# First two weight tiles of four projections take each normalised chunk together

## What is computed

```
def swiglu(x, w13, w2):
    gate, up = jnp.split(x @ w13, 2, axis=-1)
    return (jax.nn.silu(gate) * up) @ w2
...
x = layer_norm(DEEPNORM_ALPHA * x + (1.0 + g_m) * y, ln_mix_g[i], ln_mix_b[i])
u = x * (1.0 + sc_f) + sh_f
y = swiglu(u, ffn_w13[j], ffn_w2[j])
...
x = x + mod_l[5] * swiglu_2(modulate(rms_norm(x, norm2_w[i]), mod_l[3], mod_l[4]), ffn_w1[i], ffn_w3[i], ffn_w2[i])
```

## Time and profile before

| | |
|---|---|
| three executions | 2711.41, 2708.13, 2701.3 us |
| profiled execution, span (the page gives no other time for it) | 2713.5 us |
| PE busy | 2625.8 us, 97% |
| POOL, DVE, ACT busy | 910.4, 909.8, 404.2 us |
| mean granted PE clock | 0.989 |

### The profile page before, as it was taken

The page is one execution under the profiler, slowest core; times in us unless marked ns, Lnnn a source line. Parts: engine busy times, 40 slices in busy tenths (PEclk is TensorE's granted clock), DMA queues, the critical chain, the costliest instruction groups (busy, mean ns, idle before and its releaser), DMA issues.

```text
span 2713.5 us, 47220 instructions
## 1 busy us (share of the span) xinstructions
PE 2625.8 (97%) x20645; PEld 1863.1 (69%) x20645; DVE 909.8 (34%) x1647; ACT 404.2 (15%) x839; POOL 910.4 (34%) x715
## 2 busy tenths in 40 slices
PE   8999999989999999999999999999999999999998
PEld 6767799956644444334445446488888778998998
DVE  4746422384300011100013583222221136522651
ACT  0132010120311000100002344100000121221000
POOL 2662168584000000000000350145555331612886
PEclk9999999999999999999999999999999999999999
DMA  9978545478499999999997210323222243122552
GB/s 299 320 250 287 135 162 164 149 264 280 156 376 407 407 381 385 391 399 406 385 384 249 79 38 16 124 78 93 80 83 86 89 129 109 58 67 93 171 163 87
DMA packets 318303, 561.88 MB, mean 207 GB/s; under 512 B 45544, under 2 KB 181520, under 8 KB 317968
## 3 DMA queue, kind: packets, MB, share of 16 engines
q1 hardware_dynamic: 299280, 554.57, 57.4%
q10 hardware_dynamic: 18816, 4.27, 0.8%
HBM read 557.75 MB, written 1.05 MB: 206 GB/s over the span
## 4 chain that ended last, share of the span: by engine, by line
PE 50%; issue 36%; POOLq 4%; POOL 4%; DVE 2%; DVEq 1%; ACT 1%; DMA 1%; SPq 0%; ACTq 0%
PE psum L1937 10%; PE psum L2166 5%; PE psum L1974 5%; PE psum L2020 4%; PE psum L1021 3%; PE psum L1406 3%; PE psum L2194 2%; PE psum L1359 2%; PE psum L2040 2%; PE psum L1753 2%; POOLq L3767 2%; PE psum L1419 1%; PE psum L2067 1%; PE psum L1244 1%; PE psum L1062 1%
## 5 line engine op out<-in xcount | busy, mean ns | idle before, releaser
L1614 PE MATMUL psum<-ring,xe 128*32 128x512 f32 (+1 forms) x4608 | 458.0, 557 | 2.0 <-issue 1.4
L1614 PEld LDWEIGHTS psum<-ring,xe 128*32 128x32 f32 x4608 | 156.4, 110 | 291.1 <-issue 255.4
L3906 POOL TENSOR_TENSOR ckv<-ckv,nstat 128x512 f32<-128x512 f32 x2 | 2.5, 1265 | 889.9 <-DVE nstat L3413 889.9
L3304 DVE TENSOR_TENSOR act_in<-act_in,psum 128x256 f32<-128x256 f32 (+1 forms) x72 | 28.7, 399 | 629.5 <-ACT act_in L2474 629.5
L1636 PE MATMUL psum<-ring,zs 128*32 128x256 f32 x4224 | 232.3, 379 | 0.2 <-DMA ring<-in_moe_w 0.2
L1636 PEld LDWEIGHTS psum<-ring,zs 128*32 128x32 f32 x4224 | 141.7, 110 | 92.7 <-issue 5.5
L3919 POOL TENSOR_TENSOR w_sums<-ring 128x512 f32<-128x512 f32 (+1 forms) x34 | 42.4, 1247 | 298.1 <-DVE ctxT L3470 124.1
L2474 ACT ACTIVATE act_in<-psum 128x256 f32<-128x256 f32 (+1 forms) x72 | 26.4, 367 | 567.9 <-PE psum L1614 567.9
L1753 PE MATMUL psum<-a,ring 128*128 128x512 f32 x224 | 97.5, 594 | 2.0 <-ACT a L2523 1.3
L3413 DVE RECIPROCAL nstat<-nstat 128x512 f32<-128x512 f32 x23 | 75.8, 3328 | 43.0 <-ACT nstat L2235 43.0
L1937 PE MATMUL psum<-a,w_sums 128*128 128x256 f32 x352 | 83.2, 379 | 2.0 <-ACT a L2523 2.0
(11 more groups left out here) (612 smaller groups left out, 4892.6 us busy)
## 6 DMA issues: line engine op xcount, KB each, us to landing
ring<-in_moe_w SPq DMA_DIRECT2D x216, 1024.0 KB, 11.2
ring<-in_ffn_w SPq DMA_DIRECT2D x97, 1024.0 KB, 5.2
ring<-in_ada_w SPq DMA_DIRECT2D x96, 1024.0 KB, 8.4
ring<-in_moe_w SPq DMA_DIRECT2D x64, 768.0 KB, 6.6
ring<-in_hg_w_in SPq DMA_DIRECT2D x20, 1024.0 KB, 5.1
ring<-in_mlstm_w_in SPq DMA_DIRECT2D x16, 1024.0 KB, 9.2
ring<-in_mlstm_w_out SPq DMA_DIRECT2D x8, 1024.0 KB, 7.7
ring<-in_s_w_glu SPq DMA_DIRECT2D x8, 1024.0 KB, 11.7
```

What stands on the lines that cost most here:

```text
L1614: last = pe.matmul(psum[rows, r, 0:2 * nb * 32].rearrange("p (u b f) -> p u b f", u=2, b=nb), xe[:, k, at:at + 32], tile[:, :, :, rows], s ...
```

## The change

The first two weight tiles of the four projections are interleaved: PE waits for a chunk and multiplies it with tile 0 and tile 1 before it waits for the next. In `ffn0` all of tiles 0 and 1 is done so. In `ffn2` and `hg` products 1, 2 and 3 of both tiles are, and in `ffn3` products 1 and 2; the remaining products of tile 0 follow, then those of tile 1. The spare products between chunks are gone. Tile 1 of `ffn3` writes to other banks. On ACT the SiLU of tile 0 of `ffn0` now stands ahead of the S5 exponentials, and on DVE the product of gate and up ahead of the S5 parameters.

```diff
         def gate_up_side3(n):
-            return 2 * ((n + 1 - (job_of["rms3"] + 2) % NB // 2) % 2)
+            return NB if n == 1 else 2 * ((n + 1 - (job_of["rms3"] + 2) % NB // 2) % 2)
...
-                for n in range(2):
-                    mm_pair(ffn_tile(n), ffn_job(n), lambda k: act_in[:, k],
-                            before=None if n else lambda k: pe.wait_ge(S("ffn0_in_ready"), k + 1))
+                def first_tiles():
+                    for n in range(2):
+                        wait_tile(pe, ffn_tile(n))
+                        wait_free(pe, ffn_job(n))
+                    for k in range(DC):
+                        pe.wait_ge(S("ffn0_in_ready"), k + 1)
+                        for n in range(2):
+                            for b in range(2):
+                                at = k * 2 * P + b * P
+                                last = pe.matmul(bank(ffn_job(n))[:, b * T:(b + 1) * T], ring[:, ffn_tile(n) % RING, at:at + P],
+                                                 act_in[:, k], start=k == 0 and b == 0, stop=k == DC - 1, skip_group_check=True)
+                                if b == 0 and k == n * (DC - 1):
+                                    last.then_inc(tile_begun, 1)
+                            if k == DC - 1:
+                                full(last, ffn_job(n))
...
+                def first_two():
+                    for n in range(2):
+                        wait_tile(pe, t0 + n)
+                    for m in (1, 2, 3):
+                        if m == 3:
+                            pe.wait_ge(S("w_sums_ready"), INPUT_TILES - PLAIN_TILES + FF_SEVENS + 2)
+                            pe.wait_ge(S("a2_ctx_ready"), 16)
+                        for k in range(4):
+                            if m != 3:
+                                pe.wait_ge(S("a2_lat_ready"), 8 + (0 if m == 1 else 4) + k + 1)
+                            for n in range(2):
+                                last = product(n, m, k)
...
+                    for n in range(2):
+                        for m in (5, 6, 7, 4):
+                            if n == 0:
+                                pe.wait_ge(S("x_sums_ready"), 4 + 4 + {5: 1, 6: 2, 7: 3, 4: 4}[m])
+                            elif m == 6:
+                                pe.wait_ge(S("gap_mods_out"), 2)
+                            for k in range(4):
+                                last = product(n, m, k)
...
-                            if n == 0 and (m, k) in ((1, 2), (2, 0)):
-                                spare_products(product_bank(1, 1)[:, 0:P], 3 if m == 1 else 7)
...
-                s5_exponentials()
                 wait_full(act, ffn_job(0))
                 out_of(act.activation(sil[:, 0].rearrange("p a t -> p (a t)"), bank(ffn_job(0)), ACT.Silu), ffn_job(0))
+                s5_exponentials()
...
-                s5_parameters()
                 wait_out(dve, ffn_job(0))
                 wait_full(dve, ffn_job(1))
                 out_of(dve.tensor_tensor(hid[:, 0], sil[:, 0], bank(ffn_job(1)).rearrange("p (a t) -> p a t", a=2), ALU.mult),
                        ffn_job(1))
+                s5_parameters()
```

More of the change, by code:

```diff
@@ L1910, in gate_up @@
                 def gate_up(n):
                     wait_tile(pe, t0 + n)
[L1913 to L1924, removed]
@@ L1925, in gate_up @@
-                    for m, (held, moving) in operands.items():
+                    pe.wait_ge(S("quads_out"), n - 1)
+                    for m in operands(n):
                         if m == 3:
                             pe.wait_ge(S("w_sums_ready"), INPUT_TILES - PLAIN_TILES + FF_SEVENS + n + 1)
-                        if n == 0 and m in (5, 6, 7, 4):
-                            pe.wait_ge(S("x_sums_ready"), 4 + 4 + {5: 1, 6: 2, 7: 3, 4: 4}[m])
                         for k in range(4):
-                            if n == 0 and (m, k) in ((1, 2), (2, 0)):
-                                spare_products(product_bank(1, 1)[:, 0:P], 3 if m == 1 else 7)
[L1933 to L1937, removed]
+                            last = product(n, m, k)
@@ L1982, in down @@
                             last.then_inc(S("quads_full"), 1)
-                for n in range(N_GATE_UP):
+                first_two()
+                for n in range(2, N_GATE_UP):
                     gate_up(n)
@@ L2025, in forget_tile @@
                     last.then_inc(S("quads_full"), 1)
-                for i in range(8):
+                first_two()
+                for i in range(2, 8):
                     forget_tile(i)
@@ new lines, in product, with first_two @@
+                def product(n, m, k):
+                    held, moving = operands(n)[m]
+                    return pe.matmul(small_bank(gate_up_side3(n), m), held[:, k], moving(k), start=k == 0, stop=k == 3)
+                def first_two():
+                    for n in range(2):
+                        wait_tile(pe, t0 + n)
+                    for m in (1, 2):
+                        for k in range(4):
+                            pe.wait_ge(S("a2_lat_ready"), 24 + (0 if m == 1 else 4) + k + 1)
+                            for n in range(2):
+                                last = product(n, m, k)
+                                if (m, k, n) == (1, 0, 0):
+                                    last.then_inc(tile_begun, 1)
+                    for n in range(2):
+                        for m in (6, 5, 7, 3, 4):
+                            if m == 6:
+                                pe.wait_ge(S("w_sums_ready"), INPUT_TILES - PLAIN_TILES + FF_SEVENS + QUADS_3 + n + 1)
+                            if n == 0 and m in (6, 7, 4):
+                                pe.wait_ge(S("x_sums_ready"), 4 + 4 + 8 + {6: 2, 7: 3, 4: 4}[m])
+                            for k in range(4):
+                                last = product(n, m, k)
+                                if (n, m, k) == (1, 6, 0):
+                                    last.then_inc(tile_begun, 1)
+                            if m == 6:
+                                last.then_inc(S("first_full"), 1)
+                        last.then_inc(S("quads_full"), 1)
@@ L2158, in gate_up @@
[L2158 removed]
+                    pe.wait_ge(S("quads_out"), OUT_3 + n - 1)
+                    for m in operands(n):
                         if m == 6:
                             pe.wait_ge(S("w_sums_ready"), INPUT_TILES - PLAIN_TILES + FF_SEVENS + QUADS_3 + n + 1)
[L2161 to L2162 removed]
                         for k in range(4):
[L2164 to L2166 removed]
+                            last = product(n, m, k)
```

111 lines of the change are left out of this document (72 added, 39 removed).

## The result

The kernel after took 2689.38 us (median of 4 runs, 2687.84 to 2691.78), the kernel before on the same chip 2705.82 us (4 runs, 2701.3 to 2711.41). The ratio is 0.994, with a 95% interval of 0.9928 to 0.9953: 16.2 us faster by the ratio, between 12.7 and 19.5 (the two medians lie 16.4 apart). The forecast was 2689.7.

A forecast was written before the change was run, and what follows sets the result against it. PE, busy 97% of the span, was taken as the bound, with gains where it idles or runs slow at four starts. 6.6 + 3.45 + 5.2 + 4.2 = 19.4 us, less 1, from 2708.1 gave 2689.7 us, range 2681 to 2701.

The forecast's parts named there:

- ffn0, 6.6 us: Start of `ffn0`: PE no longer starves between chunks and reaches the product needing the last input sum at 337.25, not 343.87.
- The moved multiply: DVE in `ffn0`: running at about 337.1 behind the sums, it frees a bank for tile 3 and costs no wait.
- POOL's slack: After `ffn0`: POOL's 10.2 us of waits for PE exceed the 7.35 us shift, so POOL catches up before its tight stretch.
- ffn2, 3.45 us: Start of `ffn2`: 16 records of tile 1 go between the chunks, into idle stretches and the place of spare products.
- hg, 5.2 us: Start of `hg`: 3.45 us of hidden work as in `ffn2`, plus 1.76 us from half clock gone as the gap shrinks.
- one such gap in two: `ffn2` and `hg`: a 1.99 us gap brings half clock in one case of two, at 1.76 us.
- ffn3, 4.2 us: Start of `ffn3`: ten remaining products of tiles 0 and 1 end at 2505.4 instead of 2509.58, at full clock.
- The clock term: `ffn3`: 2.4 of the 4.2 us come from full clock, kept up by twice the records between chunks.
- rival 2: Missing spares bring half clock at `ffn2` and it stays at `hg`: 2693; at `hg` alone 2691.5. Chance 0.12.
- signs of being wrong: Idle PE on `bank_out` in `ffn0`, POOL waits beyond 1 us, half clock starting `ffn2` or `hg`, first matmul awaiting a landing.
- The 1 us taken off for the clock: Whole kernel: 19.4 us cut to 18.4, since another execution need not have all the half clock of this one.
- Rival 3: `ffn0`'s gain is lost at POOL's tight stretch or the new input-sum wait: 12.8 us gained, 2695. Chance 0.10.

The follow-up runs named there:

- the other trace of the old code: Trace of the kernel after with the old `ffn0` put back, `ffn2`, `hg` and `ffn3` staying changed; ratio to the kernel before 0.9959.
- eight more sums: Kernel after plus eight dead sums on POOL ahead of the weight sums of tile 4 in `ffn0`; ratio to the kernel before 0.9975.
- sums first: Kernel after, but DVE in `ffn0` forms the input sums directly behind the chunks, before scaling `xT` and filling two buffers; ratio to the kernel before 0.9943.
- POOL's additions: Kernel after with two or eight dead sums added on POOL ahead of tile 4's weight sums in `ffn0`; ratios to the kernel before 0.9937 and 0.9975.

## Why the prediction was right

The mechanism was right at all four places: waiting and work that stood one behind the other now lie over each other. That the forecast of 2689.7 came within 0.3 us of the measured 2689.38 is partly luck. The starting point of 2708.1 was 2.3 us above the later median of 2705.82, and the gain of 18.4 was 2.0 above the 16.4 between the medians.

**ffn0, 6.6 us.** 6.61 in this pair of traces, 6.0 by the kernel with this part alone, and 5.2 against the other trace of the old code. The estimated 14 us for 64 records without idle, the two products behind them, and the new wait for `caT` came as reckoned; the wait was 0.95 us instead of 1.2. The moved multiply, counted at nothing, is worth that only where it now stands: in the old place it and the SiLU cost 6.8 us, about all that `ffn0` gains.

**POOL's slack** was the weak step, though its conclusion held. The prediction compared the sum of POOL's waits for PE, 10.2 us, with 7.35. At the tight stretch the outcome was as it said: POOL's waits fell to 3.7 us, and PE's wait stayed at 0.38. But the first use at tile 4 has a margin of its own, and the prediction did not look at it. It fell from 9.9 to 2.8 us, by 7.2, close to the 7.35. Had the change moved PE 3 us more, PE would have waited there, with POOL still idle later on, as the kernel with eight more sums shows.

**ffn2, 3.45 us**: 3.38 measured. **hg, 5.2 us**: 4.99 in this pair of traces, but 1.6 of it is the clock, and that was luck of the execution. In the kernel with `ffn0` alone the same unchanged stretch, with the same 1.99 us gap, had its half clock under the chunks, where it is hidden. So what the change gives there is about 3.4 us, and up to 1.8 more in some executions. The prediction had this as "one such gap in two", from two gaps. The gap itself shrank to 0.81 us, not to 1.1.

**ffn3, 4.2 us**: 4.12 in this pair, and 3.0 against the trace with `ffn0` alone, measured alike from the last matmuls of the modulation to tile 2 (21.91 before, 20.76 there, 17.79 after). The clock term is partly a draw here too. But one part of it recurs: the product behind the wait for `x_sums` took 3.76 and 3.70 us in the two kernels without the interleave and 2.02 us in all eight with it. The gap of 0.9 us ahead of it is the same in all ten and isn't what brings the half clock, since the clock is at half level before it in both kernels without the interleave. In the kernel before:

```profile
2494.40 1.17 PE L2166 MATMUL psum<-act_in,ring 128*128 128x128 f32 x4 [0.60 <-DVE act_in L3384]
```

Four such records take 0.81 us at full clock. The clock fell while PE took four records at a time between waits, and it didn't fall there with eight at a time. In five of the eight it had been at half level a few microseconds earlier and had come back; in the other three, as with `ffn0` alone, it was full until then. That the denser work keeps it up fits all ten traces, but was not tested by itself.

**The new waits.** That the first matmul of `ffn2` would wait for tile 1 was foreseen; it did, for 1.16 us, and in `hg` for 0.99, which was not. Both cost nothing, since the chunks behind it come later anyway: the fifth chunk is multiplied 8.58 us behind the modulation's last matmuls in `ffn2` before (the row at 1757.91 of the earlier trace rows) and 8.67 us after. The half clock did come at these starts, as rival 2 feared, but here it was hidden too. So two of the prediction's own signs of being wrong, half clock at these starts and a first matmul that waits for a landing, came true beside a right result. The second contradicted its own section on `ffn2`. They would have been better signs with a price: PE's next group late. The kernel with the sums first is the control for the clock, at `ffn2`:

```profile
1736.67 3.85 PE L1939 MATMUL psum<-a,ring 128*128 128x256 f32 x16 [1.07 <-DMA ring<-in_ffn_w]
1742.22 3.72 PE L1939 MATMUL psum<-a,ring 128*128 128x256 f32 x16 [1.70 <-DVE a L3487]
```

Here the first 16 records are at full clock, 3.85 us, and PE then waits 1.70 us; in the kernel after they took 5.38 and PE waited 0.18. Either way the next group starts 5.55 or 5.56 us behind the first. Where the half clock came behind that wait, in the kernel without the new `ffn0`, it cost 0.7 us.

**The sum.** 19.4 predicted at the four places, 19.1 found. Both come from the same trace of the kernel before, with all its half clock, so their agreement shows that the reckoning was right and not that the change is worth as much. With the other traces of the old stages it is 5.2 + 3.3 + 3.3 + 3.0 = 14.8 us. The 16.2 of the runs lies between. The 1 us taken off for the clock was the right kind of caution and too little. (Rival 3's figure of 2695 leaves that 1 us out, which the others take off.)

The missing 0.6 us between `ffn0` and `ffn2` and the 0.95 us in the later part of `hg` are no loss by the change. The S5 stage, from the row at 484.10 to the gated projection behind it (L1538), takes 135.93 us in this trace after, 134.61 before and 133.7 to 134.7 in the kernels with `ffn0` alone, old order, sums first and POOL's additions. From tile 2 of `hg` to `ffn3` it is 283.49 us after and 282.54 before, but 283.23 with `ffn0` alone, where `hg` is unchanged, and 282.54 with the spare products back.

## What to carry to other kernels

When a stage starts by waiting for its inputs piece by piece, give each piece all the work that can use it, from a second weight tile too. Then walk the engines that must follow to the first use of what each makes: the margin there decides, and the sum of their later waits doesn't replace it. Look also at who holds the result banks, since the same change with the old order on ACT and DVE lost 6.8 of its 16.2 us. And read the stage to be changed in more than one trace: the half clock moves from execution to execution, and a gain reckoned from one trace holds that trace's draw.

## What was not expected of the hardware

A gap of 1.99 us at the same place of `hg` was followed by half clock in one execution and by full clock in another, in which the half clock had come earlier. In `ffn3` the clock fell before the gap of 0.9 us, in both kernels in which PE worked in small pieces. The Trainium skill (TensorE: Matmul & The Clock Gate, Why this matters for your kernels) warns of idle gaps longer than these. It agrees with the 4.45 and 10.36 us gaps above, both followed by half clock; for the short ones, the measured rows decide: the gap alone doesn't tell, and the work ahead of it seems to count too.

DVE's operations on 128x256 took 1.86 us for two and 4.84 us for eight while POOL formed its sums, and 0.73 and 2.67 us with POOL idle, at the same place of the same code. An engine that nobody waits for can be what makes another one late.
